# Products that nobody reads, put into four pauses of TensorE in a fused diffusion layer

## The reference, cut to what matters

```
def trunk_layer(x, cond, lp, row, col, ctx_k, ctx_v, ctx_state):
    mod = jnp.einsum('bd,de->be', jax.nn.silu(cond), lp['w_mod']) + lp['b_mod']
    sh1, sc1, g1, sh2, sc2, g2 = jnp.split(mod, 6, axis=-1)
    mix, ctx_out = token_mixer(modulate(x, lp['norm1_g'], sh1, sc1), lp, row, col, ctx_k, ctx_v, ctx_state)
    x = x + g1[:, None, :] * mix
    x = x + g2[:, None, :] * hier_moe(modulate(x, lp['norm2_g'], sh2, sc2), lp)
    return x, ctx_out
...
        sa = jnp.einsum('bhvk,bhk->bhv', S, kk_t)
        S = S * w_t[:, :, None, :] - sa[..., None] * b_t[:, :, None, :] + v_t[..., None] * k_t[:, :, None, :]
        return S, jnp.einsum('bhvk,bhk->bhv', S, r_t)
...
    for e in range(N_EXPERTS):
        hid = jax.nn.silu(x @ lp['exp_gate'][e]) * (x @ lp['exp_up'][e])
        out = out + combine[:, e:e + 1].astype(x.dtype) * (hid @ lp['exp_down'][e])
```

## Time and profile before

| what | value |
|---|---|
| time, median of 3 runs | 1118.52 us (1115.24 to 1119.87) |
| profiled execution | 1115.67 us, its span 1113.9 us |
| mean granted TensorE clock | 0.938 |
| TensorE busy | 966.7 us of the span, 87% |
| VectorE / ScalarE / GpSimd busy | 423.0 / 274.5 / 81.1 us |

### The profile page before, as it was taken

How to read it: one execution, slowest core, us unless ns; L and a number is a source line. 1 busy time by engine, 2 the same in 40 slices (tenths; PEclk the granted TensorE clock), 3 DMA queues, 4 the chain that set the end, 5 groups by cost and what they waited for, 6 DMA issues and landing times. The chain is left out here.

```text
span 1113.9 us, 18522 instructions
## 1 busy us (share of the span) xinstructions
PE 966.7 (87%) x7858; PEld 568.3 (51%) x7858; DVE 423.0 (38%) x775; ACT 274.5 (25%) x518; POOL 81.1 (7%) x133
## 2 busy tenths in 40 slices
PE   3699999997887768999979982999999999999960
PEld 0265555544465557898955552444444444444420
DVE  1501652233288877687756554000000000000006
ACT  1311222223567642233230120111111111111112
POOL 0230000001000012122200003000000000000002
PEclk9999999998689987999979995899999999999995
DMA  9812435446999810133246226969899989989707
GB/s 341 274 28 71 157 104 199 152 152 241 406 406 404 322 40 17 43 84 96 70 122 250 76 76 233 346 231 347 303 346 345 336 310 350 346 312 334 287 38 282
DMA packets 98485, 247.18 MB, mean 222 GB/s; under 512 B 7524, under 2 KB 12420, under 8 KB 98160
## 3 DMA queue, kind: packets, MB, share of 16 engines
q1 hardware_dynamic: 86960, 218.64, 54.1%
q0 software_dynamic: 5632, 13.97, 4.3%
q10 hardware_dynamic: 5824, 13.55, 3.1%
HBM read 176.51 MB, written 67.01 MB: 219 GB/s over the span
## 5 line engine op out<-in xcount | busy, mean ns | idle before, releaser
L2172 PE MATMUL ps<-arena 128*128 128x512 f32 x544 | 239.2, 596 | 1.7 <-ACT arena L2222 1.7
L2172 PEld LDWEIGHTS ps<-arena 128*128 128x128 f32 x544 | 102.4, 191 | 126.6 <-issue 125.9
L2186 PE MATMUL ps<-arena 128*128 128x512 f32 x272 | 121.3, 598 | 3.6 <-ACT arena L2226 3.6
L697 PE MATMUL ps<-arena 128*128 128x512 f32 (+3 forms) x448 | 123.6, 435 | 0.0
L697 PEld LDWEIGHTS ps<-arena 128*128 128x128 f32 (+1 forms) x448 | 67.7, 188 | 60.2 <-issue 59.3
L2186 PEld LDWEIGHTS ps<-arena 128*128 128x128 f32 x272 | 50.7, 192 | 62.1 <-issue 62.1
L1841 PE MATMUL ps<-arena 128*128 128x512 f32 x160 | 73.6, 613 | 1.9 <-PEq L1310 1.9
L2263 DVE TENSOR_TENSOR arena<-arena,ps 128x512 f32<-128x512 f32 x17 | 11.7, 688 | 136.9 <-ACT arena L2218 136.9
L564 DVE SCALAR_TENSOR_TENSOR arena<-arena 128x128 f32<-128x128 f32 (+3 forms) x56 | 30.9, 552 | 82.6 <-ACT arena L440 81.1
L2271 DVE COPY arena<-ps 128x512 f32<-128x512 f32 x17 | 11.8, 692 | 125.8 <-PE ps L2186 125.8
L2222 ACT ACTIVATE arena<-ps 128x1024 f32<-128x1024 f32 x18 | 18.4, 1024 | 140.8 <-PE ps L2164 140.8
(11 more groups left out here) (311 smaller groups left out, 1323.9 us busy)
## 6 DMA issues: line engine op xcount, KB each, us to landing
gathered_tokens<-arena SPq DMA_DIRECT2D x16, 2560.0 KB, 26.5
arena<-in_exp_up_dram SPq DMA_DIRECT2D x17, 2048.0 KB, 18.0
arena<-in_exp_gate_dram SPq DMA_DIRECT2D x17, 2048.0 KB, 13.0
arena<-in_exp_down_dram SPq DMA_DIRECT2D x17, 2048.0 KB, 9.9
arena<-in_w_mod_dram SPq DMA_DIRECT2D x12, 2048.0 KB, 14.0
arena<-gathered_tokens SPq DMA_DIRECT2D x18, 512.0 KB, 15.2
expert_outputs<-arena ACTq DMA_DIRECT2D x17, 512.0 KB, 8.2
arena<-in_w_in_dram SPq DMA_DIRECT2D x4, 2048.0 KB, 8.0
```

Of the source, the lines that this page charges most:

```text
L697: mm = pe.matmul(ps[0:m, b, 0:hi - lo], ring[:, slot_of(what), k, (e % 4) * P:(e % 4) * P + m], hT[:, k, lo:hi], start=(k == 0), stop=(k = ...
L2172: mm = pe.matmul(ps[:, b, :], xgT[:, k, :], w[u][:, k, :], start=(k == 0), stop=(k == KT - 1))
L2186: mm = pe.matmul(ps[:, Y0 + half, :], hidT[:, k, :], wd[u][:, k, half * 512:(half + 1) * 512], start=(k == 0), stop=(k == 3))
```

## The change

A helper makes `times` products of the identity matrix with itself repeated four times (128 by 128 by 512), into a PSUM bank whose content nobody reads at that time. It is called in five places of TensorE's list, in four pauses: four products at the end of the attention block, behind a wait for `first_out`; one before `inner(0)`, behind a wait for `m_ok`; one before and six behind the last `ranks`; and two at the start of the expert block. Nothing waits for them, and the other engines' lists are as before.

```
+        def keep_running(pe, bank, times):
+            for _ in range(times):
+                pe.matmul(ps[:, bank, :], ident, ident.unsqueeze(1).to_broadcast([P, 4, P]), start=True, stop=True)
...
                 mm.then_inc(cpv_mm, 1)
+                pe.wait_ge(first_out, 1)
+                keep_running(pe, 0, 4)
...
                 diag_blocks(pe, 7, (BY - 1, BY), 1).then_inc(m_mm, 1)
+                pe.wait_ge(m_ok, 1)
+                keep_running(pe, BDIAG, 1)
                 inner(0)
                 inverse(0)
...
                 route_logits(4)
+                keep_running(pe, 6, 1)
                 ranks(1, 3, NTT)
+                keep_running(pe, 6, 6)
...
                     pe.nop().then_inc(one, 1)
+                keep_running(pe, Y0, 2)
                 x_turn(0, 0, 16)
                 gate_up(0, 0, 32)
```

## The result

The changed kernel takes 1111.3 us (median of 6 runs, 1109.11 to 1116.19) where the kernel before, timed beside it, takes 1119.19 us (6 runs, 1115.24 to 1120.56). The ratio is 0.9946, with a 95% interval of 0.9922 to 0.9969: some 6 us less. They differ by up to 0.2% from the quotient of the two medians, which here is 0.9930, or 7.9 us.) I had forecast 1116.2 us, 2.3 us less.

A forecast was written before the change was run, and what follows sets the result against it. The kernel was taken as mostly TensorE's own time, half clock costing only where its products are waited for. Scan's start 1.0 us plus router and experts 1.3 us, taken from 1118.52 us, gave 1116.2 us, range 1112.0 to 1120.0 us.

The forecast's parts named there:

- The price of a product: One added product on TensorE takes 0.88 us at full clock and 1.75 us at half clock.
- The four products behind attention: At the change to the scan block: no cost, a new 2.7 us pause for the states, gain at most 0.37 us.
- The product before `inner(0)`: At the scan's start: may restore clock in 429 to 436 us; 2.5 us at best, 1.0 us taken.
- slower: Rival: the product before `inner(0)` delays the scan's chain by 0.9 to 1.8 us; 1119.4 to 1120.3 us, 10 in 100.
- The products at router and experts: Between router and experts: no cost; 3.1 us if the clock holds, 0 to 2.2 if it falls; 1.3 taken.
- the two at the experts' start: Before `x_turn`: no cost; if the clock fell, they help it rise a little earlier, 0 to 2.2 us.
- upper end: Router and experts, warm from 694.39: 0.93 us in `x_turn` and 2.18 us in `gate_up`, 3.1 us together.
- The sum: Scan's start 1.0 us plus router and experts 1.3 us: 2.3 us less, from 1118.52 to 1116.2 us.
- all of it works: Rival: full clock at both the scan's and the experts' start, 2.5 + 3.1 = 5.6 us; 1112.9 us, 12 in 100.
- low end: Whole kernel: all works, 1112.9 us, less 0.9 us for the scatter of runs: 1112.0 us.
- the half per cent: Whole kernel: about 0.5% (5.6 us) is what measurement can tell from none; faster by more was given 0.10.
- The rule of the Trainium skill: Clock changes come after different product counts in each run, so a median would show part of 5.6 us at best.

The follow-up runs named there:

- tail_only: Against the kernel before, only the four products behind attention are added; 1119.52 us, ratio 1.0002.
- start_only: Against the kernel before, only the two products at the start of the expert block are added; 1115.37 us, ratio 0.9968.
- scan_small: Against the kernel before, four products behind attention and one before `inner(0)`, each 32 columns wide instead of 512, none at router and experts; 1118.31 us, ratio 0.9992.
- six_only: Against the kernel before, only the one product before and the six behind the last `ranks` are added; 1119.85 us, ratio 1.0011.
- changed_again: The changed kernel itself, measured once more beside the kernel before; 1110.76 us, ratio 0.9939.
- inner_only: Against the kernel before, only the one product before `inner(0)`, behind its wait for `m_ok`, is added; 1113.9 us, ratio 0.9945.
- inner_start: Against the kernel before, only the product before `inner(0)` and the two at the experts' start are added; 1109.92 us, ratio 0.9936.
- scan_both: Against the kernel before, four products behind attention and one before `inner(0)`, none at router and experts; 1113.96 us, ratio 0.9962.
- scan_end: inner_start plus four half-width products in the waits of the scan's last step and one full-width behind its outputs; 1108.85 us, ratio 0.9894 to the kernel before.
- all_fills: scan_end and last_three together; 1107.21 us, ratio 0.9881 to the kernel before.
- inner_two: inner_start with two products before `inner(0)` instead of one; 1111.41 us, ratio 0.9917 to the kernel before.
- last_three: inner_start plus three products between the last tile's `h_turn` and its `down`; 1110.9 us, ratio 0.9905 to the kernel before.
- first two groups: Two of the three groups of four follow-up kernels; each group ran on one chip together with the kernel before.
- third group: Last of the three groups of four follow-up kernels: inner_two, last_three, scan_end and all_fills; ratios to the kernel before 0.9917, 0.9905, 0.9894 and 0.9881.

## Why the prediction was right and where its sizes were off

*The price of a product* (0.88 us warm, 1.75 at half clock): four took 3.70 us, two at half clock 3.75 us, against 3.5 forecast for both, and the six 6.92 us against 7.0. Right.

*The four products behind attention*: "this part costs nothing", and a new pause of 2.7 us for the states "in which the clock may fall just as well". Right: 2.79 us, and alone they gave 1.0002. In the execution profiled after, the clock held through that pause; in tail_only it fell behind it. That the four ran at full clock in the one after was luck: attention's tail before them was at half clock up to 409.

*The product before `inner(0)`*: the mechanism (less half clock behind it) was right as far as the traces show, the size was not, and this is the step that was mis-sized. I wrote that "this place gives 2.2 + 0.37, some 2.5 us at best" and took 1.0 us. Alone it gives 6 us (0.9945). The 2.2 us of the sum were worked out from the 7 us at half clock that one execution showed. That execution was a favourable one. The working also put the 1.30 us of "issue" within `inverse(0)` at nothing, and no execution with the product has a pause of over 0.4 us there. Step 1 in the profiled executions:

| kernels | step 1, us |
|---|---|
| without the full product before `inner(0)`: before, start_only | 14.61, 14.28 |
| the same: tail_only, scan_small, six_only | 18.01, 18.02, 18.08 |
| with it: changed, changed_again, inner_only, inner_start, scan_both, scan_end, all_fills, inner_two | 12.23, 12.57, 13.01, 12.31, 12.52, 12.59, 12.58, 12.49 |
| with it: last_three | 14.07 |

So the step takes 14.3 to 14.6 or 18.0 us without the product, and 12.2 to 14.1 with it. Against 18.0 us the gain is some 5.6 us in this step alone, against 14.5 us some 2. The times fit, though they don't fall into two groups: of the 61 runs of the kernel before beside the first two groups 24 were above 1120 us, of 36 of tail_only, scan_small and six_only 16, and of 40 with the product (inner_only, scan_both, changed_again, inner_start) none. How often the step of 18 us comes in the kernel before is not known, since it was profiled once. My rival "slower" (0.9 to 1.8 us on the path) had its price right, 1.06 us in the profile after, and its condition was met, but what it bought was larger: from the start of `inner(0)` to the copy of step 0's right sides it is 3.9 to 4.7 us with the product and 5.5 to 6.3 us without, so the head got no longer.

*The products at router and experts*: that the clock rises in the six and is lost in the pause behind them was right (1.00 at 679 to 685, 0.50 from 686), and six_only shows that they are worth nothing. Wrong was how I weighed the two at the experts' start: I let them give "0 to 2.2 us" if the clock had fallen, and took 1.3 us. Cold as they were, they and `x_turn` behind them brought it back before `gate_up` in each of the eight profiled executions that have them: first tile 17.45, 17.39, 17.15 and 17.15 us (changed, start_only, changed_again, inner_start) and 17.16 to 17.85 us in the third group, against 20.24, 20.26, 19.66, 19.71, 19.79 and 19.72 us without them (before, tail_only, inner_only, scan_small, six_only, scan_both). That is 1.8 to 3.1 us where I took 1.3, and 3.1 was my upper end.

*The sum*: 2.3 us forecast, some 6 us measured; the case "all of it works" (5.6 us, 12 in 100) is what came, with other sizes in it. The median of 1111.3 us lies 0.7 us under the low end that I gave; by the ratio, from the 1118.52 us that I started from, it is 1118.52 x 0.9946 = 1112.5 us, just inside. That it lies inside is luck in part: the gain is more than twice what I forecast, it is at the half per cent past which I gave 1 in 10, and both terms of the sum were too small.

*The rule of the Trainium skill* (page "TensorE: Matmul & The Clock Gate", its section on the clock gate), that the point of change is not tied to the kernel's start: the runs agree, with step 1 of kernels that are the same up to there at 14.3 and at 18.1 us (start_only, six_only), and attention's last 14 us at half clock in one execution and not in another. But I drew the wrong conclusion from it. I let it cut the gain of the change; by the same rule the one execution before was one draw, and what it did not show was the step of 18 us, which none of the nine profiled executions with the product has.

## What to carry to other kernels

A product that nobody reads pays where TensorE's next work is alone on the path and the clock would be low in it: right before that work, in a wait that has room for it, rather than at the start of the pause. The six fillers with 5.3 us of pause left behind them were lost; the three that left 1.0 us of a pause of 3.6 us were followed by full clock in both executions that have them. Before such a change is sized, read several executions: the clock's changes move from one to the next, and one trace shows one outcome.

## What the runs showed of the hardware that I had not expected

TensorE can be busy by the profile and stay at 1.2 GHz: 17.16 of 18 us in tail_only at a clock of 0.53, all in products of the scan, 32 to 128 columns wide. With one product of 128 by 128 by 512 before `inner(0)`, 1.06 us long at full clock, six of nine profiled executions had no half clock from it to the end of step 1, and three had some 7 us of it. Without it, or with one of 32 columns in its place, two of five had some 7 us and three had 17 us. Whether the product's work does this or the 0.9 us that it takes is open, as said above. And the same program, on the same chip, took 1113.6 to 1124.3 us in 34 runs, with a mean granted clock from 0.941 to 0.924, the lower ones in the longer runs.
